# The half-empty column pair of the input projection changes places with the second pair of S5 inputs

## The reference

```
for l in range(2):
    h = rms_norm(x, norm_g[l])
    z = h @ w_in[l]                                  # 4096 x 10064
    (s5_u, s5_gate, mla_cq, mla_ckv, mla_kr, mla_gate, gla_q, gla_k, gla_v,
     gla_glr, gla_gate, lru_u, lru_gate) = split_cols(z)
    y = [s5_mixer(s5_u), mla_mixer(cq, ckv, kr), gla_mixer(q, k, v, glr), rglru_mixer(lru_u)]
    x = x + concat(normed and gated y) @ w_out[l]
return rms_norm(x, final_g)
```

## Time and profile before

| what | value |
|---|---|
| median of 3 runs | 2877.06 us (2876.66 to 2879.03) |
| the profiled execution | 2878.85 us |
| its span, first to last instruction | 2877.1 us |
| mean granted TensorE clock | 0.993 |
| busy: PE, DVE, ACT, POOL | 97%, 69%, 55%, 26% |
| DMA, mean | 182 GB/s |

### The profile page before, as it was taken

One profiled execution on the slowest core, in us unless ns is written; L12 is line 12 of the kernel. 1 busy time (PEld: TensorE's weight loads), 2 busy tenths in 40 slices (PEclk: granted clock), 3 DMA queues, 4 the chain that ended last, 5 costly groups with the idle time before them and its releaser, 6 DMA issues.

```text
span 2877.1 us, 55833 instructions
## 1 busy us (share of the span) xinstructions
PE 2804.0 (97%) x16152; PEld 2410.4 (84%) x16152; DVE 1992.2 (69%) x3284; ACT 1571.8 (55%) x2812; POOL 745.6 (26%) x813
## 2 busy tenths in 40 slices
PE   6999999999999999999999999999999999999997
PEld 4878888888888888888877888888888888888886
DVE  8799999755555567555577999986555555755555
ACT  5555555655566565444455555556566555644443
POOL 3255555300001023111123545551001010411111
PEclk9999999999999999999999999999999999999998
DMA  6765656655555556777746565656555555577775
GB/s 225 227 186 177 184 175 183 180 166 159 165 156 169 164 149 201 217 210 209 206 142 190 173 186 175 186 173 179 166 155 168 163 154 157 168 211 217 209 210 175
DMA packets 276413, 522.65 MB, mean 182 GB/s; under 512 B 30913, under 2 KB 33873, under 8 KB 275281
## 3 DMA queue, kind: packets, MB, share of 16 engines
q1 hardware_dynamic: 257360, 477.13, 56.0%
q10 hardware_dynamic: 18944, 44.18, 4.8%
HBM read 508.60 MB, written 16.78 MB: 183 GB/s over the span
## 4 chain that ended last, share of the span: by engine, by line
PE 45%; DVE 2%; issue 2%; ACT 1%; POOL 0%; DVEq 0%; ACTq 0%; POOLq 0%
PE ps L294 26%; PE ps L293 13%; PE ps L443 1%; DVE w L973 1%; PE ps L326 1%; PE ps L456 0%; PE ps L452 0%; PE ps L296 0%; DVE zb L1512 0%; PE ps L337 0%; DVE yy L1042 0%; PE ps L304 0%; PE ps L465 0%; PE ps L464 0%; ACT w L590 0%
## 5 line engine op out<-in xcount | busy, mean ns | idle before, releaser
L294 PE MATMUL ps<-hb,w 128*128 128x512 f32 x5824 | 2053.0, 396 | 7.3 <-POOL hb L1542 6.1
L973 DVE TENSOR_TENSOR w<-raw,w 128x512 fp32r<-128x512 f32 x1760 | 1290.0, 740 | 789.6 <-ACT w L590 780.5
L590 ACT ACTIVATE w<-raw 128x512 fp32r<-128x512 f32 x1760 | 1092.9, 628 | 1035.3 <-PE ps L294 1034.3
L293 PE MATMUL ps<-hb,w 128*128 128x256 f32 x5690 | 1623.9, 285 | 13.8 <-DVE w L973 12.7
L294 PEld LDWEIGHTS ps<-hb,w 128*128 128x128 f32 x5824 | 1092.8, 188 | 251.4 <-issue 6.7
L293 PEld LDWEIGHTS ps<-hb,w 128*128 128x128 f32 x5690 | 1076.6, 189 | 57.0 <-DVE w L973 28.4
L294 PE MATMUL ps<-gl,w 128*128 128x512 f32 x640 | 226.7, 395 | 0.0
L1693 POOL TENSOR_TENSOR nf<-zb 128x256 f32 (+1 forms) x60 | 51.9, 864 | 537.2 <-DVE zb L1480 531.7
L294 PE MATMUL ps<-w,hb 128*128 128x512 f32 x512 | 179.1, 393 | 0.0
L293 PE MATMUL ps<-gl,w 128*128 128x256 f32 x560 | 156.6, 280 | 0.0
L1546 POOL TENSOR_TENSOR sx<-yl 128x256 f32<-128x256 f32 x16 | 15.6, 975 | 504.2 <-DVE yl L1346 504.2
(11 more groups left out here) (299 smaller groups left out, 2470.1 us busy)
## 6 DMA issues: line engine op xcount, KB each, us to landing
raw<-in_w SPq DMA_DIRECT2D x1763, 256.0 KB, 2.8
mlaw<-in_mlaw ACTq DMA_DIRECT2D x16, 768.0 KB, 4.2
mlaw<-in_mlaw ACTq DMA_DIRECT2D x16, 512.0 KB, 3.5
gate<-xres ACTq DMA_DIRECT2D x32, 256.0 KB, 4.3
xres<-zb ACTq DMA_DIRECT2D x32, 256.0 KB, 3.6
zb<-in_x SPq DMA_DIRECT2D x8, 512.0 KB, 7.3
xres<-in_x SPq DMA_DIRECT2D x4, 1024.0 KB, 6.5
s5w<-in_s5w ACTq DMA_DIRECT2D x16, 256.0 KB, 2.7
```

The lines of the kernel that those rows point to most:

```text
L293: mm(acc[:, T:], a_lo, m_hi, start=False, stop=False, skip_group_check=True)
L294: last = mm(acc, a_hi, m_both, start=(k == 0), stop=(k == nk - 1), skip_group_check=True)
L590: A(w2[:, d, :, 0, :], raw[:, s, :, :], ACT.Copy).then_inc(hi_ready, 1)
L973: V.tensor_tensor(w2[:, d, :, 1, :], raw[:, s, :, :], w2[:, d, :, 0, :].bitcast(F), ALU.subtract).then_inc(w2_ready, 1)
```

## The change

In the order of columns, the second pair of S5 inputs (tiles 4 to 7) and the pair with the half-empty half change places. Pair 1 now computes the two `cq` tiles and then `kr`, `glr` and zeros; pair 2 computes S5 inputs 4 to 7. The steps between the chunks keep their pairs and their places: the parameter work stays in pair 1, the first S5 iteration in pair 2. The number of chunks, of loads and of matmuls stays the same.

```
@@ tensor
-                pre_pair(1, {29: lambda: s5_in(l * G8, 0)})
-                pre_pair(2, s5_steps(l * G8, first=True), one=True)
+                pre_pair(1, {29: lambda: s5_in(l * G8, 0)}, one=True)
+                pre_pair(2, s5_steps(l * G8, first=True))
@@ scalar
                 pre_pair(1, {0: [lam_exponent], 2: [turn_sines], 25: [lambda: s5_inputs(l * G8, 0)],
-                             31: [lambda: s5_tables(l * G8, 0)]})
+                             31: [lambda: s5_tables(l * G8, 0)]}, one=True)
                 own.restart()
-                pre_pair(2, s5_steps(l * G8, 0), one=True)
+                pre_pair(2, s5_steps(l * G8, 0))
@@ vector
-                def pre_pair(i, steps, one=False):
+                def pre_pair(i, steps, dst=None):
...
-                            if one and h == 1:
-                                evac(h_l + (i * 2 + h), h, kg.unsqueeze(1), 1)
-                            else:
-                                evac(h_l + (i * 2 + h), h, zb[:, bass.ds(i * 4 + 2 * h, 2), :])
-
-                pre_pair(1, {0: [s5_turns], 4: [s5_scale], 6: [s5_scale2], 14: [lru_softplus]})
+                            z = zb[:, bass.ds(i * 4 + 2 * h, 2), :] if dst is None else dst[h]
+                            evac(h_l + (i * 2 + h), h, z, z.shape[1])
+
+                pre_pair(1, {0: [s5_turns], 4: [s5_scale], 6: [s5_scale2], 14: [lru_softplus]},
+                         dst=(zb[:, Z_LATENT[0]:Z_LATENT[0] + 2, :], kg.unsqueeze(1)))
                 own.restart()
-                pre_pair(2, s5_steps(l * G8, 0, first=True), one=True)
+                pre_pair(2, s5_steps(l * G8, 0, first=True),
+                         dst=(zb[:, Z_S5 + 4:Z_S5 + 6, :], zb[:, Z_S5 + 6:Z_S5 + 8, :]))
@@ host
-    pre = np.concatenate([s5u, cq[:, :CC], kr, glr, pad, qk, lruu, cq[:, CC:], ckv, gv[:, :3 * CC]], axis=1)
+    pre = np.concatenate([s5u[:, :2 * CC], cq[:, :CC], kr, glr, pad, s5u[:, 2 * CC:], qk, lruu, cq[:, CC:], ckv, gv[:, :3 * CC]], axis=1)
```

## The result

| | before | after |
|---|---|---|
| median of 5 runs | 2876.67 us (2876.07 to 2879.03) | 2862.91 us (2861.31 to 2863.51) |
| the profiled execution | 2878.85 us | 2863.51 us |
| its span | 2877.1 us | 2861.7 us |

The ratio is 0.9949 with a 95% interval of 0.9938 to 0.9960: 13.8 us faster by the medians, 15.4 by the spans. The forecast was 2860.5 us and a gain of 16.5 us.

What follows compares the result with a forecast made beforehand. Matmuls on TensorE, busy 97% of the span, were taken as the bound. Gains of 8.32 us in layer two and 8.22 in layer one, together 16.5, took 2877.06 to 2860.5 us, range 2855.5 to 2867.

Steps and rivals of the forecast that it cites:

- short half: Pair 1's second half, newly half-empty: 12.41 us floor plus 1.86 us for softplus, 14.27 us.
- The old half is idle, and the idle time is recoverable: Pair 2's second half, layer two: matmuls and S5 input product need 12.41 us against 21.26, so 8.85 us are lost.
- The engines' pace carries 0.693 us a chunk: New short half: VectorE splits 0.60 us apart, ScalarE 0.52, both under 0.693 us a chunk; cost nothing.
- Softplus costs 1.86 us: Start of the new short half: TensorE waits 1.23 and 0.41 us for splits, plus restarts; bounds nothing to 3.0 us.
- Pair 3's first half loses its excess: Pair 3's first half falls from 26.03 to 24.71 us, since VectorE no longer enters it late.
- entering the loop: Rival: pair 3's first half keeps its extra 1.32 us because of the loop's entry, 2863.1 us; chance 0.1.
- Pair 2's first half keeps its 23.92: Pair 2's first half, directly after the new short half, stays at 23.92 us.
- The loads cost nothing: New short half: nothing taken in layer two or one, with 1 us as layer one's upper end.
- a few tenths: Loads at 0.885 us a chunk would be short only at the very end of the short half, by this much.
- the opening's 411 GB/s: Load rate in the opening stretch, 0.64 us a chunk, taken over the page's 358 GB/s, an estimated 0.732 us.
- In layer one it just fits: Chunk 24's load, behind a 1 MB copy of x, lands at 109.3 us and is rounded at 109.8.
- The clock stays up: New short half keeps 1.00; the rival, a fall there, costs 1.7 us in each layer, 2863.9 us; chance 0.1.

Runs made afterwards that it cites:

- before_half_loads: The kernel before, with its half-empty halves loading only the used column tile, rounding and subtraction as wide as before: 2877.99 us, ratio 1.0001.
- before_narrow: The kernel before, with its half-empty halves loading and splitting only the used column tile: 2871.92 us, ratio 0.9977.
- after_calm: The changed kernel with softplus at c = 10 of pair 1 and the copies of x moved to chunks 112 to 160: 2859.01 us, ratio 0.9934.
- after_again: The changed kernel measured once more, without a further change: 2862.35 us, ratio 0.9947 to the kernel before.
- before_both_tiles: The kernel before, with both column tiles multiplied in its half-empty half, the second product being unused padding: 2880.19 us, ratio 1.0008.
- after_table12: The changed kernel with the first rotation table at c = 12 of pair 1 and not at c = 31: 2866.17 us, ratio 0.9961.
- after_all: The changed kernel with softplus at c = 10, later copies of x, and short halves loading and splitting only the used tile: 2858.89 us, ratio 0.9932.

## Why the prediction was right, step by step

Sums of the four halves of the forecast, in its own terms:

| term | forecast | first profile, layer one / two |
|---|---|---|
| short half | 14.27 | 14.25 / 14.17 |
| pair 2, first half | 23.92 | 24.14 / 25.56 |
| pair 2, second half | 23.50 | 23.50 / 23.50 |
| pair 3, first half | 24.71 | 24.80 / 24.78 |
| sum | 86.40 | 86.69 / 88.01 |

- *The old half is idle, and the idle time is recoverable.* Right; shown by the two kernels with both tiles. That loads were not its cause is shown by before_half_loads; that the splits and S5 steps on VectorE are, before_narrow shows in part.
- *The engines' pace carries 0.693 us a chunk.* Right for the running chunks, wrong by 0.26 us at the start: with whole loads and splits the half takes 12.66 and 12.68 us (after_calm), because chunk 19 is split behind the evacuation. Only with narrow splits too it takes 12.39 and 12.41.
- *Softplus costs 1.86 us.* Over the floor the half took 1.84 and 1.76 us, but softplus is not the whole of it: without it layer two still takes 12.67, so softplus itself is 1.5 us. The forecast read its wait 0.2 us too long, and what it called softplus includes the evacuation's wait, which stays when softplus goes. That the sum of 14.27 came out within 0.1 us is in part luck.
- *Pair 3's first half loses its excess*: right, 24.8 us, so it came from the old place in front of it and not from entering the loop.
- *Pair 2's first half keeps its 23.92.* Too low by 0.2 us even where the loads hardly show: 24.14 and 24.15, and 24.12 with narrow loads and splits. There the table at c = 31 stands behind a short half, and its wait goes when the table is made early (23.50 to 23.8 us).
- *The loads cost nothing.* Nearly so in three of the four layers profiled (with narrow loads the short half took 0.2 us less, 13.99 and 14.00), but mis-sized in the fourth. The bound of "a few tenths" at the very end was the right place. In the first profile's layer two the price came a half later, 25.56 us where after_again has 24.15: some 1.4 us, because the table stands behind the late rounding and VectorE's S5 steps behind the table. The step of the forecast behind it was to let the opening's 411 GB/s decide: in the dense stretch the loads moved 352 and 351 GB/s. The opening has larger loads among its own and an idle TensorE; which of the two makes the difference was not tried. The DMA: Bandwidth & Descriptors page of the Trainium skill, Bandwidth, gives about 358 GB/s as a core's share of the HBM. The dense stretch lies beside it with 352, the opening above it with 411. That share is meant for both cores of a pair at work, and here one runs, so the nearness doesn't show what bound the loads. Nor does the rate alone make the price, since after_again ran at the same one; the buffers hid it there, as the forecast said.
- *In layer one it just fits.* True of the changed kernel alone, and by the grace of softplus.
- *The clock stays up.* Right, at 1.00, with waits of 1.04 and 0.40 us. With one of 2.47 us in the same place it did not always (see the last section).

Together the four halves gained 7.93 us in layer one and 6.71 in layer two, 14.64 in all for 16.54. The span gained 15.4. The other 0.7 us come from the stretch between the layers, where nothing was changed: 1322.00 us before and 1321.32 after from the end of these halves to the start of pair 1's second half in layer two. It is no gain of the change, since before_both_tiles, with the old order, has 1320.80 there. The medians differ by 1.6 us less than the spans, because the profiled execution of before lies 2.2 us above its median and that of after 0.6. So the forecast is 1.1 us too low by the span (2860.6 against 2861.7) and 2.4 by the median (2860.5 against 2862.91), and part of the closeness is scatter: the halves that it reckoned with gained 1.9 us less than it said, and 0.7 of that came back where nothing was changed. The changed kernel taken once more gained 15.4 us by the medians of its group.

## What to carry to other kernels

A half with half of the work is worth its length only where the engines that feed it have nothing else; look for it in the stretch where they are idle, not in the order of the columns. A supply that just fits behind a stall no longer fits when the stall is taken out: moving softplus alone gained nothing in layer one until the copy of x moved too (14.77 us, then 12.66), and making the table early cost 0.8 us of the short half until the splits were narrow (13.45, then 12.42). And price a fast stretch by the load rate of an equally dense stretch with loads of the same size, and ask what stands behind the first instruction that would be late.

## What the runs showed of the hardware

- *The clock can fall behind a wait of 2.5 us, and needn't.* after_table12 has the same wait in both layers, 2.47 and 2.48 us. In windows of the short half the mean clock is 0.90 in layer one, (1 - 0.90) x 16.90 x 2 = 3.4 us at 1.2 GHz, and 1.00 in layer two; the halves take 16.90 and 15.77 us. What TensorE did in the half up to the wait was the same. In before_narrow a wait of 2.5 us drew no fall either, and in the kernel before the one of 3.02 us did.

```profile
104.48:121.38 16.90, 14.43 (x75) 11.64 (x73) 14.38 (x29) 9.89 (x17) 3.10 (x7) 0.90 0.75 249
1515.09:1530.86 15.77, 13.06 (x75) 10.48 (x74) 14.32 (x29) 10.19 (x18) 3.05 (x7) 1.00 0.70 229
```

- *Halves without idle time come in two lengths, or nearly.* Pair 2's second half takes 23.50 or 23.83 us, pair 3's first about 24.8 or 25.0, pair 1's first 22.2 or 22.6, with the same instructions and a clock of 1.00; after_all has one in layer one and the other in layer two. It is spread over the chunks, 0.02 us each. No cause was found; a difference of 0.3 us in a single half means nothing here.
- *Landing under load.* Loads of 256 KB landed after 2.6 us when nothing had moved for 2 us and after 6.5 us with the queue full (medians of two and of three), within one half.
